# Encoder trunk on one core: x kept as a sum for the output projection, the projection in smaller parts, the root of x computed earlier

## What is computed

```python
h = rmsnorm(x, norm_mix[0])
qkv = h @ w_qkv                      # q, k and v, 8 heads, two maps of 64 each per head
q = partial_rope(rmsnorm(q, q_gain), cos, sin); k = likewise
a = softmax(q0 k0^T) - lam * softmax(q1 k1^T)
o = rmsnorm(a @ v, sub_gain) * (1 - lambda_init)
x = x + o @ w_o                      # the addition that the change touches
x = x + square(relu(rmsnorm(x, norm_mlp[0]) @ w1)) @ w2
```

## Time and profile before

| | |
|---|---|
| median of 3 runs | 989.43 us |
| profiled execution | 990.6 us, span 988.8 us |
| TensorE busy | 972.1 us, 98% of the span |
| VectorE busy | 848.7 us, 86% |
| ScalarE busy | 458.4 us, 46% |
| GpSimd busy | 357.2 us, 36% |
| granted TensorE clock | 1.00 |
| DMA | 92.23 MB, mean 93 GB/s |

### The profile page before, as it was taken

One profiled execution on the slowest core, in us unless ns is written; L12 is line 12 of the kernel. 1 busy time (PEld: TensorE's weight loads), 2 busy tenths in 40 slices (PEclk: granted clock), 3 DMA queues, 4 the chain that ended last, 5 costly groups with the idle time before them and its releaser, 6 DMA issues.

```text
span 988.8 us, 12852 instructions
## 1 busy us (share of the span) xinstructions
PE 972.1 (98%) x4714; PEld 799.4 (81%) x4714; DVE 848.7 (86%) x1132; ACT 458.4 (46%) x703; POOL 357.2 (36%) x317
## 2 busy tenths in 40 slices
PE   8999999979999999999999999999999999999998
PEld 7787777767887888888888888988888888888886
DVE  6696898898787899999989988779998988989883
ACT  6435554656646353443535433475355253453520
POOL 6841454121155539376543000550440413405000
PEclk9999999999999999999999999999999999999999
DMA  7242220130252233332333241304332333422202
GB/s 262 86 109 84 65 69 18 43 128 12 75 170 86 86 107 107 107 107 86 109 104 107 86 154 39 128 1 128 86 128 86 107 107 90 123 86 86 86 1 86
DMA packets 51398, 92.23 MB, mean 93 GB/s; under 512 B 8316, under 2 KB 9352, under 8 KB 51336
## 3 DMA queue, kind: packets, MB, share of 16 engines
q1 hardware_dynamic: 45888, 91.24, 29.4%
q10 hardware_dynamic: 5448, 0.17, 0.3%
HBM read 89.30 MB, written 2.10 MB: 92 GB/s over the span
## 4 chain that ended last, share of the span: by engine, by line
PE 91%; DVE 3%; POOL 3%; issue 1%; ACT 1%; DMA 0%; ACTq 0%; DVEq 0%; POOLq 0%
PE bank L1678 44%; PE pair L1678 43%; PE pair L1739 1%; PE bank L1739 1%; DVE s_nmax L1316 1%; POOL s_ropet L623 1%; POOL s_ropet L622 1%; DVE s_acc L1517 0%; DMA s_x_nat<-in_x 0%; PE bank L2029 0%; POOL s_ropet L612 0%; ACT s_p L975 0%; DVE s_acc L1555 0%; PE bank L1841 0%; PE pair L2017 0%
## 5 line engine op out<-in xcount | busy, mean ns | idle before, releaser
L772 POOL TENSOR_TENSOR s_lt<-s_lbB,s_lbB 128x1024 f32<-128x1024 f32 x14 | 33.6, 2402 | 258.2 <-PE pair L1678 161.7
L1200 DVE TENSOR_TENSOR s_lbB_lo<-s_lbB,s_b_hi 128x1024 fp32r<-128x1024 f32 x64 | 122.0, 1928 | 3.4 <-ACT s_b_hi L873 3.4
L1173 DVE TENSOR_TENSOR s_w_lo<-s_raw,s_w_hi 128x1024 fp32r<-128x1024 f32 x72 | 120.3, 1690 | 5.0 <-ACT s_w_hi L851 5.0
L873 ACT ACTIVATE s_b_hi<-s_lbB 128x1024 fp32r<-128x1024 f32 x64 | 67.2, 1053 | 81.4 <-POOL s_lbB L772 39.3
L1678 PE MATMUL bank<-s_hT_hi,s_w_hi 128*128 128x512 f32 x256 | 100.2, 392 | 0.0
L1678 PE MATMUL pair<-s_hT_hi,s_w_hi 128*128 128x512 f32 x256 | 100.1, 391 | 0.0
L1678 PE MATMUL bank<-s_hT_hi,s_w_lo 128*128 128x512 f32 x256 | 99.6, 389 | 0.0
L1678 PE MATMUL pair<-s_hT_hi,s_w_lo 128*128 128x512 f32 x256 | 99.6, 389 | 0.0
L1678 PE MATMUL bank<-s_hT_lo,s_w_hi 128*128 128x512 f32 x256 | 99.6, 389 | 0.0
L1678 PE MATMUL pair<-s_hT_lo,s_w_hi 128*128 128x512 f32 x256 | 99.6, 389 | 0.0
L1034 ACT ACTIVATE s_u_raw<-s_u_raw 128x512 f32<-128x512 f32 x64 | 40.4, 632 | 110.6 <-DVE s_u_raw L1419 110.6
(11 more groups left out here) (268 smaller groups left out, 2676.8 us busy)
## 6 DMA issues: line engine op xcount, KB each, us to landing
s_raw<-in_mlp_w SPq DMA_DIRECT2D x64, 512.0 KB, 3.7
s_lbB<-in_mlp_w SPq DMA_DIRECT2D x64, 512.0 KB, 3.3
s_raw<-in_attn_w_qkv SPq DMA_DIRECT2D x24, 512.0 KB, 3.7
s_raw<-in_attn_w_o SPq DMA_DIRECT2D x8, 512.0 KB, 3.3
s_x_nat<-in_x SPq DMA_DIRECT2D x4, 512.0 KB, 6.3
s_x_again<-in_x SPq DMA_DIRECT2D x4, 512.0 KB, 7.5
out<-s_acc SPq DMA_DIRECT2D x8, 256.0 KB, 2.0
s_raw<-in_pool_w SPq DMA_DIRECT2D x4, 256.0 KB, 2.8
```

Of the source, the lines that this page charges most:

```text
L772: g.tensor_tensor(w2_raw[n][:], w2_raw[one][:], w2_raw[two][:], ALU.subtract).then_inc(t_done, 1)
L873: a.activation(b_hi[home][:], w2_raw[n][:], ACT.Copy).then_inc(w2_hi_done, 1)
L1173: v.tensor_tensor(w_lo[slot][:, cols], raw[k][:], f32(w_hi[slot][:, cols]), ALU.subtract)\
L1200: v.tensor_tensor(w2_lo[n][:], w2_raw[n][:], f32(b_hi[home][:]), ALU.subtract).then_inc(w2_lo_done, 1)
```

## The change

The output projection's fillers come in parts of one or more heads' shares, each with its step (`W_O_PARTS`), and there are 8 of them instead of 16. Chunks 4 and 7 include head 4. x is not loaded again and not turned again: GpSimd adds `hT_hi` and `hT_lo` of a chunk into `x_kept`, in place of `hT_hi`, in the steps of `X_SUMMED` (behind the work on a head's output of that step), and VectorE adds it to the projection's chunk straight from the bank. ScalarE's copy is gone. The splits of slabs 5, 6 and 7 have other steps. The root of x stands behind the second of the angle's steps instead of behind the tables, and the sine stands behind ScalarE's first two scaled copies. At the start the first x tile is loaded in two halves with the first weight piece between them, 4 dummy turns stand in place of 12, tile 1 is turned before the first matmuls, and the low parts of h are made in another order (`H_AT`). Shortened:

```diff
 ADDED = (0, 7, 11, 17)
-F_V, F_Y, F_END = 8, 12, 28
-def y_filler(f):
-    four, k = divmod(f - F_Y, 4)
-    return ("w_o", "x")[k // 2], 2 * four + k % 2
+F_V, F_Y, F_END = 8, 12, 20
+W_O_PARTS = (
+    ((18, (0,)), (19, (1,)), (21, (2,)), (22, (3,))),
+    ((19, (0,)), (21, (1,)), (22, (2,)), (23, (3,))),
+    ((23, (0,)), (24, (1,)), (26, (2, 3))),
+    ((25, (0, 1)), (26, (2,)), (27, (3,))),
+    ((27, (0, 1)), (28, (2, 3)), (29, (4,))),
+    ((29, (0, 1, 2, 3)),),
+    ((30, (0, 1, 2)), (31, (3,))),
+    ((31, (0, 1, 2)), (32, (3,)), (33, (4,))))
+X_SUMMED = (17, 22, 22, 25, 25, 26, 29, 30)
+W_O_DONE = [parts[-1][1][-1] + 1 for parts in W_O_PARTS]
 def filler_steps():
     at = {(u // 2, u % 2): u * 11 // 16 for u in range(2 * F_V)}
     at |= {(F_V + u // 2, u % 2): 11 + u * 7 // 8 for u in range(2 * (F_Y - F_V))}
-    w_o = ((18, 22), (20, 22), (24, 24), (25, 26), (27, 28), (28, 29), (31, 31), (32, 32))
-    turned_x = (23, 23, 26, 27, 30, 30, 33, 33)
     for f in range(F_Y, F_END):
-        what, c = y_filler(f)
-        at |= {(f, u): w_o[c][u] if what == "w_o" else turned_x[c] for u in range(2)}
+        at |= {(f, u): step for u, (step, _) in enumerate(W_O_PARTS[f - F_Y])}
     return at
 FILL = filler_steps()
-TAKE = {f: FILL[f, 1] + 1 for f in range(F_END)}
+TAKE = {f: max(step for (g, _), step in FILL.items() if g == f) + 1 for f in range(F_END)}
 TAKE |= {f: max(TAKE[f], TAKE[F_V - 1] + 2) for f in range(F_V, F_Y)}
-SPLIT = {4: (0, 1, 2, 3), 5: (5, 6, 7, 8), 6: (15, 16, 18, 19), 7: (27, 28, 29, 30), 8: (34, 34, 35, 35)}
+SPLIT = {4: (0, 1, 2, 3), 5: (4, 6, 7, 7), 6: (13, 14, 15, 19), 7: (27, 28, 31, 33), 8: (34, 34, 35, 35)}
 LAST = STEPS + 6
 MAP_BANKS = 2
...
             xv = x.rearrange("a (t p) d -> p (a t) d", p=P)
+            sp.dma_start(x_nat[:, 0, 0:BANK], xv[:, 0, 0:BANK]).then_inc(x0_half_loaded, 16)
             for t in range(NT):
-                sp.dma_start(x_nat[:, t, :], xv[:, t, :]).then_inc(x_loaded[t], 16)
+                if t:
+                    sp.dma_start(x_nat[:, t, :], xv[:, t, :]).then_inc(x_loaded[t], 16)
                 sp.dma_start(raw[t][:].rearrange("p (a b) -> p a b", a=2), piece(0, t)).then_inc(raw_loaded[t], 16)
+                if t == 0:
+                    sp.dma_start(x_nat[:, 0, BANK:D], xv[:, 0, BANK:D]).then_inc(x_loaded[0], 16)
...
                     load(s, k, piece(s, k))
-            wait_used(sp, WO0 - 1)
-            for t in range(NT):
-                sp.dma_start(x_again[:, t, :], xv[:, t, :]).then_inc(x_again_loaded[t], 16)
...
                 axpy(low, TWO_PI, turns_, low)
+                pool.wait_ge(v_done, 1)
+                g.tensor_tensor(in_r[:], in_v[:], minus_half[:, 0:NT], ALU.pow).then_inc(r_done, 1)
                 for n, shift in enumerate((0.0, math.pi / 2)):
...
             rope_tables()
-            pool.wait_ge(v_done, 1)
-            g.tensor_tensor(in_r[:], in_v[:], minus_half[:, 0:NT], ALU.pow).then_inc(r_done, 1)
...
                         .then_inc(o_normed, 1)
+                for c in range(NC):
+                    if X_SUMMED[c] == i:
+                        pool.wait_ge(proj_done, NT * WO0)
+                        g.tensor_tensor(x_kept[:, c, :], f32(hT_hi[:, c, :]), f32(hT_lo[:, c, :]), ALU.add)\
+                            .then_inc(x_summed, 1)
                 for f in range(F_V):
...
             for t in range(NT):
-                h_hi(2 * t)
+                if t != 1:
+                    h_hi(2 * t)
                 if t == 0:
                 h_hi(2 * t + 1)
+                if t == 0:
+                    h_hi(2)
                 if t == 1:
...
             for t in range(NT):
-                if t == 3:
-                    act.wait_ge(rope_reduced, 1)
-                    a.activation(ropet[:, 2:4, :], ropet[:, 0:2, :], ACT.Sin).then_inc(rope_act, 1)
                 split_hi(1, t, 1)
...
                         split_hi(3, t, 1)
+                    if s == 0 and t == 2:
+                        act.wait_ge(rope_reduced, 1)
+                        a.activation(ropet[:, 2:4, :], ropet[:, 0:2, :], ACT.Sin).then_inc(rope_act, 1)
                     if s == 1:
...
             for i in range(LAST + 1):
-                for f in range(F_Y, F_END):
-                    what, c = y_filler(f)
-                    if TAKE[f] == i and what == "w_o":
-                        act.wait_ge(wo_ready, c + 1)
-                        a.activation(y_part[:, c, :], bank[6 + f % 2][:], ACT.Copy).then_inc(y_kept, 1)
                 if 2 <= i < STEPS + 2:
...
-            for t in range(NT):
+            h_lo(0)
+            dve.wait_ge(pos_turned, 1)
+            v.tensor_copy(posf[:], bank[2][:, 0:NT]).then_inc(pos_known, 1)
+            split_lo(0, 0, 0)
+            h_lo(2)
+            h_lo(1)
+            split_lo(0, 1, 0)
+            h_lo(3)
+            for t in (2, 3):
                 h_lo(2 * t)
...
                 for f in range(F_Y, F_END):
-                    what, c = y_filler(f)
-                    if TAKE[f] == i and what == "x":
-                        dve.wait_ge(y_kept, c + 1)
-                        dve.wait_ge(x_turned, c + 1)
-                        v.tensor_tensor(y_part[:, c, :], y_part[:, c, :], bank[6 + f % 2][:], ALU.add)\
+                    if TAKE[f] == i:
+                        c = f - F_Y
+                        dve.wait_ge(x_summed, c + 1)
+                        dve.wait_ge(wo_ready, c + 1)
+                        v.tensor_tensor(y_part[:, c, :], bank[6 + f % 2][:], x_kept[:, c, :], ALU.add)\
                             .then_inc(wo_added, 1)
...
             def turn_in(t):
-                pe.wait_ge(x_loaded[t], 16)
                 for half in range(2):
                     n = 2 * t + half
+                    if n == 0:
+                        pe.wait_ge(x0_half_loaded, 16)
+                    else:
+                        pe.wait_ge(x_loaded[t], 16)
                     if n >= 4:
-                        pe.wait_ge(h_lo_done, n - 3)
+                        pe.wait_ge(h_lo_done, max(H_AT[k] for k in range(n - 3)) + 1)
                     for c in range(4):
...
             nc.tensor.transpose(bank[2][:, 0:NT], pos_rows[0:NT, :], ident[0:NT, 0:NT]).then_inc(pos_turned, 1)
-            keep_turning(12)
+            keep_turning(4)
+            turn_in(1)
             pe.wait_ge(w_hi_done, 1)
                 mm(bank[0][:], hT_lo[:, c, 0:P], w_hi[0][:, c * BANK:(c + 1) * BANK])
-            turn_in(1)
             pe.wait_ge(w_lo_done, 1)
...
                     elif g >= F_Y:
-                        what, c = y_filler(g)
-                        pe.wait_ge(y_kept if what == "w_o" else wo_added, c + 1)
-                what, c = ("projection", 0) if f < F_Y else y_filler(f)
+                        pe.wait_ge(wo_added, g - F_Y + 1)
+                c = f - F_Y
...
+                    for k in W_O_PARTS[c][part][1]:
+                        pe.wait_ge(w_lo_done, 4 * WO0 + k + 1)
+                        pe.wait_ge(side_lo_done, SIDE_NO["o", k] + 1)
+                        last = w_o_part(dst, c, k, k == 0, k == W_O_DONE[c] - 1)
+                    if k == W_O_DONE[c] - 1:
+                        last.then_inc(wo_ready, 1)
...
+            def w_o_rest(cs, ks):
+                for c in cs:
+                    for k in ks:
...
+                        if k >= W_O_DONE[c]:
+                            last = w_o_part(bank[c], c, k, k == W_O_DONE[c], k == NH - 1)
...
```

66 lines of the change are left out of this document (23 added, 43 removed).

## The result

The changed kernel takes 991.42 us (median of 20 runs, 990.16 to 993.98) beside 989.55 (20 runs, 988.86 to 990.69) of the kernel before: a ratio of 1.0021, 95% interval 1.0014 to 1.0027. That is 1.9 us slower; the forecast was 6.7 faster. Its executions also lie further apart, 3.8 us against 1.8 (see the end).

A forecast was written before the change was run, and what follows sets the result against it. TensorE was taken as the bound, with gaps only in the first 36 us and from 191.75 to 262.81. Root 1.9, start 0.8 and tail 4.0 summed to 6.7, giving 982.7 us; own range 981 to 984.5, 8 in 10 979.8 to 986.3.

The forecast's parts named there:

- Root of x early, 1.9: TensorE's 1.94 us wait for the first scaled copy at 36.27 would go whole, with GpSimd's power moved earlier.
- Nothing stands in its place that I can find: No other wait would replace the 1.94 us removed at 36.27; slab 1's weights would be split earlier too.
- at most 0.4: Largest loss expected for GpSimd's squares, with rope_ready at about 36.5 instead of 34.3.
- Rival C: Early root does nothing, as TensorE at slab 1 waits for Sin's table load or splits: 984.6 us, chance 0.11.
- Start, 0.8: First 12 us: halved first load and 4 dummies would gain 0.8 us, bounds -0.5 and 1.4; first matmul at 9.4.
- Attention steps, sum 65.5: Steps 18 to 31, each the larger of TensorE's work and VectorE's loop, would total 65.5 us against 66.5.
- only the sums of steps 20 and 24 fall where VectorE sets the step: Attention stage: reason for charging GpSimd's eight sums of x only 0.8 us of VectorE time, bounds 0 and 5.5.
- Rival D: GpSimd's eight sums in the attention stage set VectorE's pace, 1.48 us each: slower, 993.7 us, chance 0.05.
- TensorE has no free time in 36 to 191 and little after 262.81, so both pieces shift all that follows: Rest of the program: the early and tail gains would pass through to the end, 6.7 us in all.
- the tail (4.0): Attention stage to the MLP: projection in parts and no turns of x would gain 4.0 us net of sums.

The follow-up runs named there:

- run 2: Kernel before with only GpSimd's power for the root of x moved early, Sin left in its place on ScalarE: 987.70 us beside 989.58.
- run 1: Kernel before with the root of x early and Sin behind the two scaled copies, nothing else: 989.29 us beside 989.58.
- run 4: Kernel before with the tail alone (x kept as a sum, output projection in parts), old start and root: 991.64 us beside 989.58.
- run 7: run 4 with VectorE waiting for GpSimd's second difference of weights before its first low part at the MLP's start: 990.01 us.
- run 8: Kernel before with run 2's early root, run 6's tail with gated sums and run 7's ordered low part: 985.63 us.
- run 14: run 13 with the early root, Sin kept where it was: 987.24 us, 0.9966 to 0.9984 of the kernel before.
- run 5: Changed kernel with GpSimd's eight sums of x left out, a write of eight columns in place of each: 987.49 us beside 989.51.
- run 12: run 3 with the positions turned between the two halves of the first tile: 988.86 us, 0.9987 to 1.0005 of the kernel before.
- run 3: Kernel before with the new start alone: 992.03 us, 1.0009 to 1.0027 of the kernel before.
- run 9: run 6 with GpSimd's third difference of weights held until VectorE's first low part of w is done: 988.25 us beside 989.54.
- run 10: run 9 with the early root, Sin kept where it was: 987.32 us, 0.9966 to 0.9985 of the kernel before.
- run 11: run 10 with the change's new start too: 987.24 us, 0.9968 to 0.9986 of the kernel before.
- run 17: run 8 with GpSimd's fourth difference alone held until the first low part of w is done: 983.87 us beside 989.69.
- run 6: run 4 with one sum a step, each waiting for VectorE's combine of that step: 987.61 us, 0.9969 to 0.9988 of before.
- Run 13: run 6 with GpSimd's third and fourth differences held until VectorE's first partial sum of hidden rows: 989.20 us beside 989.54.

## Why the prediction was wrong

Point by point, by its own steps. In the traces the end lies 9.5 us from the forecast (+2.8 instead of -6.7). TensorE has lost 2.6 of them at the first scores, 3.9 more in steps 18 to 30, and 3.5 at the MLP's start; the rest, 0.4, went the other way.

- **Root of x early, 1.9.** The sentence "Nothing stands in its place that I can find" failed. The edit had two halves. The power's gives 1.9 alone (run 2). The other, Sin behind two scaled copies, puts a table load (1.28) and a wait of 2.1 in front of GpSimd's first square. I had seen rope_ready going to 36.5 (it came at 37.2), and set the loss on the squares at "at most 0.4"; it was 0.9 in the changed kernel and 0.12 in run 1. Even a chain that loses nothing takes part of the gain: TensorE, 1.94 earlier, meets its end near 75, where before 1.24 was in hand, and I checked only the next 20 us. Rival C named Sin's table, but for a wait at slab 1, not at 75. Run 1: 0.90 at the first scores and 0.3 in the median, instead of 1.9.
- **Start, 0.8.** No gain at its own point: +0.6 in this pair of traces, less than executions differ there. I placed the loads from a mean rate, and tile 1 came 1.3 later; and I took the first matmuls at the pace they have before. That pace doesn't go by the edit. With the old start and all 12 dummies the first two matmuls also stand 0.57 or 0.58 apart in runs 4, 7, 8 and 14, and with the new one 0.31 or 0.32 in runs 5 and 12. What sets it stays open. Not seen at all: the positions' turn stands behind the late half. Without the early root that is the larger price (runs 3 and 12).
- **Attention steps, sum 65.5.** Right for eleven of thirteen steps (18 to 30), which came within 0.4 of my list (3.76, 5.38, 3.76; 4.85, 4.36, 4.26, 4.92, 4.48, 4.32; 4.43, and 4.25 for step 22 in run 4). The two others hold 3.3 us: "only the sums of steps 20 and 24 fall where VectorE sets the step" and 0.8 for all. The sums have no gate, so they run in pairs where GpSimd falls idle, behind the normed output. I had their times right (near 192, 205, 223 and 243; they start at 190.5, 203.6, 224.2 and 242.2), but not what VectorE does there at 204 and 243: combine and, right behind it, a weight split. I counted 0.8 where one pair alone costs 1.6 (0.8 a sum, my upper bound was 0.69), and nothing for the pair at 242, in a step that I had down as TensorE's. Rival D had the mechanism, at 0.05, with all eight sums hitting; four of eight cost TensorE time.
- **The premise that gains shift through.** "TensorE has no free time in 36 to 191 and little after 262.81, so both pieces shift all that follows" is the step that cost most, 3.5 us. The wait table of before shows nothing at 312 because a_lo was done 0.14 before TensorE came. Busy share told me where TensorE has no gap, not what stands just behind it. The MLP's start took 2.5 + 1.0 of whatever came early, in runs 4, 5, 9, 10 and 11 alike, 1.9 in run 8 and still 0.95 in the best order tried (run 17).
- **The working that stands.** For the tail (4.0) run 6 shows it in the trace: TensorE comes to the MLP's first down product at 308.24, 4.19 before the 312.43 of before, of which 0.06 is there at the first scores. For the root (1.9) run 2 does. With the collisions removed the same edits give 5.8 us in the median (run 17, root and tail), beside 1.9 + 4.0 = 5.9 forecast for these two. (Run 17 also has the two new waits at the MLP's start; what those would do in the kernel before was not tried.)

What stays open: why half clock follows one wait of a given length and not another (below). Run 13's median lies 1.0 above run 9's though its trace ends 0.5 earlier, and the clocks of its single executions settle that much: the profiled one is among the three at 1.00 (987.5 to 987.7); the eight others were granted 0.996 to 0.998 and took 989.0 to 990.5.

## What to carry to other kernels

Before moving an operation that frees the bound engine, list what the bound engine will meet over the rest of the program with less than that gain in hand: not its waits, but the operands that were ready just in time. Where VectorE reads two SBUF operands and GpSimd works beside it, cost them as one engine, gate the GpSimd operation on the end of the VectorE one whose successors read PSUM, and expect the order to flip when anything ahead shifts by a microsecond. When an edit has two halves, take each alone: here one half carried all the gain and the other took more than half of it back.
